# Gate and up products of a feed-forward block with the high weight against low and high input in one product of 512 columns

## The chip, the cores and the metric

The kernel runs on one core of a Trainium2 chip. The core has TensorE (matrix products into PSUM, eight banks of 512 words for each of 128 partitions), VectorE, ScalarE and GpSimd for elementwise work, and SyncE, whose queue issues nearly all loads here. The metric is the device time of one execution in microseconds. TensorE's clock is granted at one of two levels, 1.2 or 2.4 GHz; the profile gives it as a share, 0.50 or 1.00.

## The reference

Two blocks of a language model on 256 tokens of width 1024. The first is a mixer (attention beside a recurrent branch) and a gated feed-forward block, the second another mixer and a mixture of experts. The change touches the two products `h @ w_ffn_gate` and `h @ w_ffn_up`, with D_FF = 2816:

```python
def first_block(x, ...):
    ...
    x = x + rms_norm(merged @ w_o[l], norm_mix_post[l])
    h = rms_norm(x, norm_ffn_pre[l])
    f = (jax.nn.silu(h @ w_ffn_gate[l]) * (h @ w_ffn_up[l])) @ w_ffn_down[l]
    x = x + rms_norm(f, norm_ffn_post[l])
    return x
```

## The kernel before

**Split numbers.** The products of this stage run on rounded 32-bit operands (fp32r). To keep precision each operand is taken apart: a high part, which is the value rounded, and a low part, which is the value less its high part. A product is then high times high, high times low and low times high, summed in the bank (`by_parts`, lines 884 to 888, three products). The input h, transposed to 8 blocks of 128 features by 256 tokens, is held as `hT_hi[1]` (high) and `hT_lo` (low, in the place of `hT`).

**Weights.** Gate and up weights come through a ring of three slots in SBUF. A slot c holds 256 columns of gate and 256 of up, 2 MB, which is tiles f = 2c and 2c + 1; there are 11 slots, 22 tiles (KF = 22). A slot is loaded when TensorE is through with the slot three before. ScalarE writes its high part in two halves into one of three buffers (`high_parts`, line 1888), VectorE then its low part in place (`low_parts`, over line 603), 2048 words each. The slots of the down projection follow in the same ring.

**TensorE.** For tile f it makes 16 groups of three products: gate into the left half of a bank, 256 columns of the bank's 512, up into the right half. So a tile has one bank, `("ff", f)`. Banks are dealt out in a fixed list (`plan_banks`), each key the next bank of eight in turn; a key waits (`write`) until the bank's holder before it has been emptied. The down projection uses four banks, `("dn", i, n)`, and waits for all four before its first product. It also waits for `f_low`, which GpSimd writes from `f_high`.

**ScalarE and VectorE.** For each tile ScalarE takes silu of the gate half out of the bank (line 2116); VectorE multiplies it with the up half (line 2803) and the bank is free. After every second tile ScalarE rounds the two results to `f_high` (line 2121), then makes the high part of a slot three further on, and VectorE its low part. Both engines go through their lists strictly in that order. The high part of a slot can't begin before its load has landed, and the next tiles stand behind its low part on VectorE.

Of the kernel before, what the change touches and what calls it, by code (L numbers as in the profile page):

```python
# [21 lines left out]
F32 = mybir.dt.float32  # L22
# [7 lines left out]
P = 128  # L30
# [144 lines left out]
def plan_banks():  # L175
# [29 lines left out]
    o += [("mg", dm) for dm in range(KD)]  # L205
    o += [("mo", i, n) for i in range(NT) for n in range(2)]
    o += [("ad", 5)] + [("hT", 1, kk) for kk in range(4)] + [("ad", 4), ("as", 5), ("as", 4)]
    o += [("ff", m) for m in range(KF)]
    o += [("dn", i, n) for n in range(2) for i in range(NT)]
    o += [("ad", 10)] + [("x2", 0, c) for c in range(4)] + [("ad", 11), ("uz", 0, 0)]  # L210
    o += [("x2", 1, c) for c in range(4)] + [("as", 10), ("uz", 1, 0)]
# [112 lines left out]
def build(nc, A, out):  # L324
    BANK = plan_banks()
    ctx = ExitStack()
    with ctx:
# [22 lines left out]
        hT = sb("hT", [P, KD, SEQ])  # L350
        small = sb("small", [P, 616 - KD * 36 - 36 - 3 * SH - KD])
        crowded = sb("crowded", [P, 1], I32)
        ring = sb("ring", [P, RING, SLOT])
        words = nc.sbuf_bytes_remaining // 4 - 16
        arena = sb("arena", [P, words])
        where = place(words)
# [66 lines left out]
        hT_hi = {n: rounded(f"h{n}_high", [KD, SEQ], "arena", where[f"hh{n}"][0]) for n in (0, 1, 2, 3)}  # L423
        hT0_lo, hT3_lo = (rounded(f"h{n}_low", [KD, SEQ], "arena", where[f"hl{n}"][0]) for n in (0, 3))

        v_hi = [rounded(f"v_high{n}", [KD // 2, 512], "arena", where[f"hv{n}"][0]) for n in range(2)]
        osb_hi, osb_lo, orw_hi, orw_lo = (rounded(n, [PAIRS, SEQ], "arena", where[b][0]) for n, b in (
# [43 lines left out]
        def write(pe, key):  # L471

            b, turn = BANK[key]
            if turn:
                pe.wait_ge(bank_free[b], turn)
            return bank[b]

        def full(key):
            return bank_full[BANK[key][0]], 1

        def filled(eng, key):

            b, turn = BANK[key]
            eng.wait_ge(bank_full[b], turn + 1)
            return bank[b]
# [10 lines left out]
        def cols(w, c0, c1):  # L496
            return w[:, c0:c1].rearrange("(k p) c -> p k c", p=P)
# [28 lines left out]
        for c in range(KF // 2):  # L526
            if c == 1:
                modulation(4)
            stream(("ff", c), [(0, cols(A["w_ffn_gate"][0], c * 256, c * 256 + 256)),
                               (2048, cols(A["w_ffn_up"][0], c * 256, c * 256 + 256))], ("ff", 2 * c + 1))  # L530
        DOWN_K = (0, 2, 6, 10, 14, 18, KF)
        n_down = len(DOWN_K) - 1
        for c in range(n_down):
# [107 lines left out]
        def _(sp):  # L641
# [24 lines left out]
            for n, (key, parts, last) in enumerate(W):  # L666
# [37 lines left out]
                    sp.wait_ge(S("orw"), 1)  # L704
                    load_ada(5)
                if key == ("in2", 0):
                    filled(sp, ("ff", KF - 1))
# [122 lines left out]
        def _(pe):  # L830
# [53 lines left out]
            def by_parts(ps, a, b, start, stop):  # L884

                mm(ps, a[0], b[0], start=start, stop=False)  # L886
                mm(ps, a[0], b[1], start=False, stop=False)  # L887
                return mm(ps, a[1], b[0], start=False, stop=stop)  # L888

            def token_major_by_parts(key, wkey, i, high, low, ready):  # L890

# [479 lines left out]
            for f in range(KF):  # L1371
                c = f // 2
                halved(("ff", c))
                ps = write(pe, ("ff", f))
                w = parts_view(("ff", c), "p (g k c) -> p g k c", g=2, k=KD)
                for gu in range(2):
                    for k in range(KD):
                        if f == 0 and gu == 0:
                            normed(1, k)
                        last = by_parts(ps[:, gu * SEQ:(gu + 1) * SEQ], [x[:, gu, k, (f % 2) * P:(f % 2 + 1) * P] for x in w],  # L1380
                                        (hT_hi[1][:, k, :], hT_lo[:, k, :]), k == 0, k == KD - 1)
                last.then_inc(*full(("ff", f)))
            ps = {}
            for n in range(2):
                for i in range(NT):
# [465 lines left out]
        def _(act):  # L1851
# [219 lines left out]
            drained(act, ("mg", 0))  # L2071
            bcast(npost, A["norm_mix_post"][0], "npost_in")
            for dm in range(KD):
                act.wait_ge(S("merged"), dm + 1)
# [35 lines left out]
            high_parts(N_FF + 1)  # L2110
            high_parts(N_FF + 2)
            for f in range(KF):
                ps = filled(act, ("ff", f))
                if f >= 2:
                    drained(act, ("ff", f - 2))
                A_(sil[:, f % 2, :], ps[:, 0:SEQ], ACT.Silu).then_inc(S("sil"), 1)
                if f % 2:

                    drained(act, ("ff", f - 1))
                    drained(act, ("ff", f))  # L2120
                    A_(fh[:, f - 1:f + 1, :], fT[:, f - 1:f + 1, :], ACT.Copy).then_inc(S("f_high"), 1)
                    high_parts(N_FF + f // 2 + 3)
            for n in range(N_FF + KF // 2 + 3, BY_TWO + 1):
# [261 lines left out]
        def _(pool):  # L2385
# [29 lines left out]
                nc.gpsimd.tensor_copy(x.rearrange("p i h t -> p (i h) t"), eye).then_inc(S("eye"), 1)  # L2415
            for dm in range(KD):
                drained(pool, ("mg", dm))
                nc.gpsimd.tensor_tensor(gates[dm], gates[dm], gates[KD + dm], ALU.add).then_inc(S("merged"), 1)

            for c in range(KF // 2):  # L2420
                pool.wait_ge(S("f_high"), c + 1)
# [11 lines left out]
        def _(dve):  # L2433
# [24 lines left out]

            def transposed_low(s, scale, bias):

                for kk in range(4):
                    ps = filled(dve, ("hT", s, kk))
                    low_seen[0] += 1
                    dve.wait_ge(S("h_high"), low_seen[0])
                    two = slice(2 * kk, 2 * kk + 2)
                    for k2 in range(2):
                        k = 2 * kk + k2
                        cols = ps[:, k2 * SEQ:(k2 + 1) * SEQ]
                        if bias:
                            ins = V.tensor_scalar(hT[:, k, :], cols, scale(k), bias(k), ALU.mult, ALU.add)  # L2470
                        else:
                            ins = V.scalar_tensor_tensor(hT_lo[:, k, :], cols, scale(k), hT_hi[s][:, k, :].bitcast(F32), ALU.mult, ALU.subtract)  # L2472
                    if bias:
                        link(ins)
                        ins = V.tensor_tensor(hT_lo[:, two, :], hT[:, two, :], hT_hi[s][:, two, :].bitcast(F32), ALU.subtract)
                    ins.then_inc(*free(("hT", s, kk)))

            def low_parts(n):
# [319 lines left out]
            low_parts(N_FF + 1)  # L2798
            low_parts(N_FF + 2)
            for f in range(KF):  # L2800
                ps = filled(dve, ("ff", f))
                dve.wait_ge(S("sil"), f + 1)
                V.tensor_tensor(fT[:, f, :], sil[:, f % 2, :], ps[:, SEQ:2 * SEQ], ALU.mult).then_inc(*free(("ff", f)))
                if f % 2:
                    low_parts(N_FF + f // 2 + 3)
            for n in range(N_FF + KF // 2 + 3, BY_TWO):
# [498 lines left out]
```

## Time and profile before

| | us |
|---|---|
| median of 3 runs | 1091.26 |
| the runs | 1089.27 to 1091.77 |
| the profiled execution | 1090.56 |
| its span (first to last instruction) | 1088.8 |
| gate and up stage | 296.0 to 422.9 |
| down projection | 422.9 to 482.9 |
| first product of the experts | about 637 |

The span is the time between the first and the last instruction of the one execution that was profiled; 1.8 us lie around it. An engine's busy time is a sum over all stages, so a stage is read from its own stretch: which engine has no gap there, and what ended the waits of the others.

### The profile page before, as it was taken

What the parts mean: (1) busy time and instruction counts of PE and PEld (TensorE: products, weight loads), DVE (VectorE), ACT (ScalarE), POOL (GpSimd) and SP (SyncE); (2) the same over time, 40 slices, a digit from 0 to 9 for tenths busy, and PEclk for the clock granted to TensorE, in tenths of its full rate; (3) what the DMA queues carried; (4) which work ended last, traced back from release to release, by engine and by line L of the source; (5) the groups of instructions that cost most, each with busy time, mean ns of one, the idle gap of its engine ahead of it and who ended that gap; (6) DMA issues with size and microseconds to landing.
All of it is one profiled execution on the core that took longest, in us unless ns stands there. A gap on an engine that the chain in (4) does not pass through costs nothing.

```text
span 1088.8 us, 17816 instructions
## 1 busy us (share of the span) xinstructions
PE 1027.2 (94%) x7505; PEld 711.6 (65%) x7505; DVE 463.3 (43%) x704; ACT 363.8 (33%) x520; POOL 59.1 (5%) x36
## 2 busy tenths in 40 slices
PE   6999999999999999999999989999999999898987
PEld 5998779899699999877996543443444343332422
DVE  5685244658653543456886341222222222121212
ACT  6562323553644443455653421111111110110102
POOL 0004310002000010000300000000000000000000
PEclk9999999999999999999999999999999999999999
DMA  9455372048765656494539999999999999999996
GB/s 322 163 200 186 110 237 82 2 164 298 235 190 159 188 162 231 158 346 140 202 119 358 422 396 410 422 420 422 422 422 422 422 422 421 422 422 421 422 419 242
DMA packets 96406, 316.37 MB, mean 291 GB/s; under 512 B 8198, under 2 KB 33110, under 8 KB 72150
## 3 DMA queue, kind: packets, MB, share of 16 engines
q1 hardware_dynamic: 95302, 313.01, 74.7%
q10 hardware_dynamic: 1040, 2.43, 0.6%
q8 instruction: 50, 0.82, 0.3%
q14 instruction: 14, 0.11, 0.0%
HBM read 314.37 MB, written 1.05 MB: 290 GB/s over the span
## 4 chain that ended last, share of the span: by engine, by line
PE 74%; DMA 17%; DVE 2%; ACT 2%; SPq 2%; issue 2%; POOL 1%; ACTq 0%; DVEq 0%; POOLq 0%
DMA arena<-in_w 16%; PE bank L1686 14%; PE bank L886 12%; PE bank L887 11%; PE bank L888 11%; PE bank L1721 6%; PE bank L1183 3%; PE bank L869 3%; PE bank L1669 2%; PE bank L1734 1%; PE bank L1099 1%; PE bank L860 1%; DMA arena<-in_ssd_norm_w 1%; PE bank L1132 1%; PE bank L1506 1%
## 5 line engine op out<-in xcount | busy, mean ns | idle before, releaser
L1686 PE MATMUL bank<-arena,hT 128*64 128x512 f32 x576 | 225.6, 594 | 3.9 <-DMA arena<-in_w 3.9
L888 PE MATMUL bank<-h_high,ring_low 128*128 128x256 f32 x680 | 193.0, 284 | 0.0
L1686 PE MATMUL bank<-ring,hT 128*64 128x512 f32 x384 | 169.3, 594 | 11.6 <-DMA arena<-in_w 11.5
L603 DVE TENSOR_TENSOR ring_low<-ring,hi_high 128x2048 fp32r<-128x2048 f32 (+2 forms) x56 | 121.9, 2217 | 98.3 <-ACT hi_high L1888 98.1
L886 PE MATMUL bank<-h_high,hi_high 128*128 128x256 f32 x536 | 153.0, 286 | 0.5 <-DVE h_low L2472 0.5
L887 PE MATMUL bank<-h_low,hi_high 128*128 128x256 f32 x536 | 151.6, 283 | 0.0
L1888 ACT ACTIVATE hi_high<-ring 128x2048 fp32r<-128x2048 f32 (+2 forms) x58 | 104.7, 1853 | 89.9 <-DMA ring<-in_w_ffn_up 39.4
L1686 PEld LDWEIGHTS bank<-ring,hT 128*64 128x64 f32 x384 | 51.4, 137 | 122.6 <-issue 98.8
L888 PEld LDWEIGHTS bank<-h_high,ring_low 128*128 128x128 f32 x680 | 131.1, 193 | 0.0
L1721 PE MATMUL bank<-arena,ac_turned 128*64 128x512 f32 x384 | 114.9, 600 | 7.5 <-issue 7.1
L3155 DVE TENSOR_TENSOR ac<-act_of,bank 128x512 f32<-128x512 f32 x16 | 17.4, 1085 | 214.6 <-ACT act_of L2316 214.6
L886 PEld LDWEIGHTS bank<-h_high,hi_high 128*128 128x128 f32 x536 | 102.7, 192 | 2.5 <-issue 2.4
L887 PEld LDWEIGHTS bank<-h_low,hi_high 128*128 128x128 f32 x536 | 102.7, 192 | 0.3 <-issue 0.2
L1686 PEld LDWEIGHTS bank<-arena,hT 128*64 128x64 f32 x576 | 69.0, 137 | 22.9 <-issue 16.4
L2316 ACT ACTIVATE act_of<-bank 128x512 f32<-128x512 f32 x16 | 9.6, 599 | 215.6 <-PE bank L1686 215.6
L1721 PE MATMUL bank<-ring,ac_turned 128*64 128x512 f32 x128 | 58.2, 609 | 4.3 <-ACT ac_turned L2320 4.3
L1721 PEld LDWEIGHTS bank<-arena,ac_turned 128*64 128x64 f32 x384 | 35.4, 138 | 41.0 <-issue 39.6
L2325 ACT ACTIVATE y_high<-con 128x512 fp32r<-128x512 f32 x31 | 19.5, 630 | 124.5 <-DVE con L3169 119.7
L3169 DVE SCALAR_TENSOR_TENSOR con<-bank,small,arena 128x512 f32<-128x512 f32 x30 | 22.5, 751 | 82.3 <-PE bank L1721 82.3
L1721 PEld LDWEIGHTS bank<-ring,ac_turned 128*64 128x64 f32 x128 | 17.2, 140 | 38.9 <-issue 37.3
L886 PE MATMUL bank<-h_high,hrw_high 128*128 128x256 f32 x144 | 41.9, 291 | 0.0
L887 PE MATMUL bank<-h_low,hrw_high 128*128 128x256 f32 x144 | 41.5, 288 | 0.0
(441 smaller groups left out, 1727.9 us busy)
## 6 DMA issues: line engine op xcount, KB each, us to landing
arena<-in_w SPq DMA_DIRECT2D x117, 1024.0 KB, 21.9
ring<-in_w SPq DMA_DIRECT2D x63, 1024.0 KB, 17.1
ring<-in_w_in SPq DMA_DIRECT2D x12, 2048.0 KB, 7.8
ring<-in_w_ada SPq DMA_DIRECT2D x8, 2048.0 KB, 8.0
ring<-in_w_ffn_gate SPq DMA_DIRECT2D x11, 1024.0 KB, 5.4
ring<-in_w_ffn_up SPq DMA_DIRECT2D x11, 1024.0 KB, 8.0
ring<-in_w_ffn_down SPq DMA_DIRECT2D x5, 2048.0 KB, 7.8
xres<-in_w SPq DMA_DIRECT2D x8, 1024.0 KB, 23.2
```

Of the source, the lines that this page charges most:

```text
L603: return eng.tensor_tensor(ring_lo[:, r, c0:c1], ring[:, r, c0:c1], high_of(n)[:, c0:c1].bitcast(F32), ALU.subtract)
L869: last = mm(ps[:, 0:512], lhs[k][:, i * P:(i + 1) * P], w[:, k, 0:512], start=(k == 0), stop=(k == nk - 1))
L886: mm(ps, a[0], b[0], start=start, stop=False)
L887: mm(ps, a[0], b[1], start=False, stop=False)
L888: return mm(ps, a[1], b[0], start=False, stop=stop)
L1183: last = mm(ps[r, j * w:(j + 1) * w], left(4 * q + j, r), right(4 * q + j, r), start=True, stop=True)
L1669: last = mm(b[:, (k % 2) * SEQ:(k % 2 + 1) * SEQ], x[i][:, k * P:(k + 1) * P], one[:, i, :], start=(i == 0 and x is x_hi), stop=(i == NT - ...
L1686: last = mm(both(6 + half, x), hg[:, k, (2 * q + x) * CAP:(2 * q + x + 1) * CAP], w13s[q][x][c][:, k % 2, half * EF:(half + 1) * EF], star ...
L1721: last = mm(both(4 + n, x), acT[:, 0, f, x * CAP:(x + 1) * CAP], w2s[q][x][f // 2][:, f % 2, n * 512:(n + 1) * 512], start=(f == 0), stop= ...
L1888: A_(high_of(n)[:, f], ring[:, r, f], ACT.Copy).then_inc(S("high"), 1)
L2325: A_(y_hi[n], y_out[:, n, :], ACT.Copy).then_inc(S("y_high"), 1)
L3169: V.scalar_tensor_tensor(y_out[:, n, :], bank[4 + n][:, :], slot_gate[:, 0:1], g2[:, n * 512:(n + 1) * 512], ALU.mult, ALU.mult).then_inc( ...
```

## The change

One product of 512 columns takes the place of two. Where `by_parts` multiplied the high weight once with high and once with low input, the two inputs are now streamed side by side: 256 columns of low, then 256 of high, against one load of the high weight. For this the low part of h is laid ahead of the high part at a fixed distance in SBUF (`hT` is allocated after the ring, and `h1_both` is a view of both), so that one access pattern of two runs of 256 words reaches both. The left half of the bank collects high weight times low input, the right half high weight times high input, and the third product, low weight times high input, is added to the right half. Gate and up of a tile now take a full bank each, `("fg", f)` and `("fu", f)`: 44 keys and two empty places in the list of banks in the place of 22 keys.

The two halves have to be added when a bank is emptied. VectorE does it with a reduce over pairs of words 256 apart: gate into `sil`, up into `fT`. ScalarE's silu reads `sil` instead of the bank, and the multiply of VectorE reads both from SBUF. A count of finished multiplies (`rows_made`, also used by the merge stage under its old name `merged`) tells ScalarE when to round.

```diff
-    o += [("ff", m) for m in range(KF)]
+    o += [(half, m) for m in range(KF) for half in ("fg", "fu")] + [None, None]
...
+            def low_beside_high(ps, w, both, high, start, stop):
+
+                def with_high_weight():
+                    return mm(ps[:, 0:2 * SEQ], w[0], both, start=start, stop=stop)
+
+                def with_low_weight():
+                    return mm(ps[:, SEQ:2 * SEQ], w[1], high, start=False, stop=False)
+
+                if stop:
+                    with_low_weight()
+                    return with_high_weight()
+                with_high_weight()
+                return with_low_weight()
...
-                ps = write(pe, ("ff", f))
                 w = parts_view(("ff", c), "p (g k c) -> p g k c", g=2, k=KD)
                 for gu in range(2):
+                    key = (("fg", "fu")[gu], f)
+                    ps = write(pe, key)
                     for k in range(KD):
                         if f == 0 and gu == 0:
                             normed(1, k)
-                        last = by_parts(ps[:, gu * SEQ:(gu + 1) * SEQ], [x[:, gu, k, (f % 2) * P:(f % 2 + 1) * P] for x in w],
-                                        (hT_hi[1][:, k, :], hT_lo[:, k, :]), k == 0, k == KD - 1)
-                last.then_inc(*full(("ff", f)))
+                        last = low_beside_high(ps, [x[:, gu, k, (f % 2) * P:(f % 2 + 1) * P] for x in w],
+                                               h1_both[k], hT_hi[1][:, k, :], k == 0, k == KD - 1)
+                    last.then_inc(*full(key))
...
             for f in range(KF):
-                ps = filled(act, ("ff", f))
-                if f >= 2:
-                    drained(act, ("ff", f - 2))
-                A_(sil[:, f % 2, :], ps[:, 0:SEQ], ACT.Silu).then_inc(S("sil"), 1)
+                drained(act, ("fg", f))
+                A_(sil[:, f % 2, :], sil[:, f % 2, :], ACT.Silu).then_inc(S("sil"), 1)
                 if f % 2:
 
-                    drained(act, ("ff", f - 1))
-                    drained(act, ("ff", f))
+                    act.wait_ge(S("rows_made"), KD + f + 1)
                     A_(fh[:, f - 1:f + 1, :], fT[:, f - 1:f + 1, :], ACT.Copy).then_inc(S("f_high"), 1)
                     high_parts(N_FF + f // 2 + 3)
...
             for f in range(KF):
-                ps = filled(dve, ("ff", f))
+                ps = filled(dve, ("fg", f))
+                V.tensor_reduce(sil[:, f % 2, :], ps.rearrange("p (h t) -> p t h", h=2), axis=AX.X, op=ALU.add).then_inc(*free(("fg", f)))
+                ps = filled(dve, ("fu", f))
+                V.tensor_reduce(fT[:, f, :], ps.rearrange("p (h t) -> p t h", h=2), axis=AX.X, op=ALU.add).then_inc(*free(("fu", f)))
                 dve.wait_ge(S("sil"), f + 1)
-                V.tensor_tensor(fT[:, f, :], sil[:, f % 2, :], ps[:, SEQ:2 * SEQ], ALU.mult).then_inc(*free(("ff", f)))
+                drained(dve, ("fu", f))
+                V.tensor_tensor(fT[:, f, :], fT[:, f, :], sil[:, f % 2, :], ALU.mult).then_inc(S("rows_made"), 1)
                 if f % 2:
                     low_parts(N_FF + f // 2 + 3)
```

Two places of the built programs show it. TensorE, from the last products of the gate and up stage to the first of the down projection; `h1_high` and `h_low` are the parts of the input, `hi_high` and `ring_low` those of the weights. Before:

```order
L888 MATMUL bank4<-h1_high_58,ring_low_70 128x256
L886 MATMUL bank4<-h1_high_58,hi_high0_49 128x256
L887 MATMUL bank4<-h_low_69,hi_high0_49 128x256
L888 MATMUL bank4<-h1_high_58,ring_low_70 128x256
L886 MATMUL bank5<-hi_high1_50,f_high_55 128x512 [waits bank_free0,low,bank_free7,f_low,bank_free6,bank_free5]
L887 MATMUL bank5<-ring_low_70,f_high_55 128x512
```

Now:

```order
L906 MATMUL bank2<-h1_both_62,hi_high0_49 128x512
L909 MATMUL bank2<-h1_both_62,ring_low_70 128x256
L906 MATMUL bank2<-h1_both_62,hi_high0_49 128x512
L909 MATMUL bank2<-h1_both_62,ring_low_70 128x256 x2
L906 MATMUL bank2<-h1_both_62,hi_high0_49 128x512
L899 MATMUL bank5<-hi_high1_50,f_high_55 128x512 [waits bank_free0,low,bank_free7,f_low,bank_free6,bank_free5]
L900 MATMUL bank5<-ring_low_70,f_high_55 128x512
```

A group of three products of 256 columns has become one of 512 and one of 256. The first product of down waits for the same four banks (5, 6, 7, 0) as before. Their last holders were tiles 14 to 17; now they are gate and up of tile 19 (banks 5 and 6) and of tile 20 (7 and 0).

VectorE, from tile 18 to tile 20; line 603 (616 in the changed kernel) is the low part of a slot, first the short first slot of down, then its second slot. Before:

```order
L603 TENSOR_TENSOR ring_low_70<-ring,hi_high1_50 128x1024 [waits high] x2
L2803 TENSOR_TENSOR arena<-arena,bank1 128x256 [waits sil,bank_full1]
L2803 TENSOR_TENSOR arena<-arena,bank2 128x256 [waits sil,bank_full2]
L603 TENSOR_TENSOR ring_low_70<-ring,hi_high2_51 128x2048 [waits high] x2
L2803 TENSOR_TENSOR arena<-arena,bank3 128x256 [waits sil,bank_full3]
L2803 TENSOR_TENSOR arena<-arena,bank4 128x256 [waits sil,bank_full4]
```

Now:

```order
L616 TENSOR_TENSOR ring_low_70<-ring,hi_high1_50 128x1024 [waits high] x2
L2828 TENSOR_REDUCE arena<-bank3 128x256 [waits bank_full3]
L2830 TENSOR_REDUCE arena<-bank4 128x256 [waits bank_full4]
L2833 TENSOR_TENSOR arena<-arena 128x256 [waits bank_free4,sil]
L2828 TENSOR_REDUCE arena<-bank5 128x256 [waits bank_full5]
L2830 TENSOR_REDUCE arena<-bank6 128x256 [waits bank_full6]
L2833 TENSOR_TENSOR arena<-arena 128x256 [waits bank_free6,sil]
L616 TENSOR_TENSOR ring_low_70<-ring,hi_high2_51 128x2048 [waits high] x2
L2828 TENSOR_REDUCE arena<-bank7 128x256 [waits bank_full7]
L2830 TENSOR_REDUCE arena<-bank0 128x256 [waits bank_full0]
L2833 TENSOR_TENSOR arena<-arena 128x256 [waits bank_free0,sil]
```

In place of one multiply that frees a bank, a tile has two reduces, which free one bank each, and a multiply that reads SBUF. The reduces of tile 20 (banks 7 and 0) stand behind the low part of down's second slot.

## Rows read from the trace of the kernel before

**Rows 1.** The page, parts 1 and 2 (PEclk: granted clock in tenths, by slice).

```profile
span 1088.8 us, 17816 instructions
...
PE 1027.2 (94%) x7505; PEld 711.6 (65%) x7505; DVE 463.3 (43%) x704; ACT 363.8 (33%) x520; POOL 59.1 (5%) x36
...
PEclk9999999999999999999999999999999999999999
```

**Rows 2.** Groups of TensorE's instructions, 294 to 430 us: busy us, mean ns.

```profile
L886 PE MATMUL bank<-h_high,hi_high 128*128 128x256 f32 x352 | 99.8, 284 | 0.5 <-DVE h_low L2472 0.5
```

**Rows 3.** Table of stretches: the gate and up stage, the down projection.

```profile
core 0: us, PE busy (x) PEld busy (x) DVE busy (x) ACT busy (x) POOL busy (x), PEclk, DMA share, GB/s
296.00:422.90 126.90, 126.90 (x1056) 126.88 (x1057) 58.60 (x50) 56.77 (x58) 12.95 (x10) 1.00 0.55 176
422.90:482.90 60.00, 60.00 (x270) 49.41 (x270) 30.03 (x23) 24.89 (x26) 1.29 (x1) 1.00 0.74 269
```

**Rows 4.** Waits of TensorE, 426 to 640; of the load queue, 500 to 1088.

```profile
PE bank L1647 <- DVE arena L3081: 1.8, 1, 1.8
...
SPq L715 <- PE bank L1099: 9.9, 1, 9.9
```

**Rows 5.** Timeline of TensorE (start, length in us): start of down, and experts.

```profile
422.78 0.28 PE L888 MATMUL bank<-h_high,ring_low 128*128 128x256 f32 x1
422.90 0.40 PE L886 MATMUL bank<-hi_high,f_high 128*128 128x512 f32 x1
423.14 0.40 PE L887 MATMUL bank<-ring_low,f_high 128*128 128x512 f32 x1
...
652.01 0.59 PE L1686 MATMUL bank<-ring,hT 128*64 128x512 f32 x1
...
652.44 0.59 PE L1686 MATMUL bank<-ring,hT 128*64 128x512 f32 x1
```

**Rows 6.** Lines of VectorE (shortest, median, longest ns); timeline of two products.

```profile
L2803 DVE TENSOR_TENSOR arena<-arena,bank x22: 406/414/420, 310.9 to 426.1; 128x256 f32<-128x256 f32 x22
...
L3159 DVE TENSOR_REDUCE small<-bank x16: 412/424/426, 656.6 to 1070.7; 128x1 f32<-128x256 f32 x16
...
L2824 DVE TENSOR_TENSOR arena<-bank,arena x4: 679/688/694, 475.2 to 483.9; 128x512 f32<-128x512 f32 x4
...
475.25 1.28 DVE L2824 TENSOR_TENSOR arena<-bank,arena 128x512 f32<-128x512 f32 x2
```

**Rows 7.** Timeline of VectorE, 318 to 336 us.

```profile
329.69 4.49 DVE L603 TENSOR_TENSOR ring_low<-ring,hi_high 128x2048 fp32r<-128x2048 f32 x2 [5.74 <-ACT hi_high L1888]
334.10 0.75 DVE L2803 TENSOR_TENSOR arena<-arena,bank 128x256 f32<-128x256 f32 x2
```

**Rows 8.** Timeline of ScalarE, 327 to 336 us, and the silu of tile 19.

```profile
327.74 3.72 ACT L1888 ACTIVATE hi_high<-ring 128x2048 fp32r<-128x2048 f32 x2 [3.06 <-DMA ring<-in_w_ffn_up]
...
334.94 0.63 ACT L2121 ACTIVATE f_high<-arena 128x512 fp32r<-128x512 f32 x1 [2.94 <-DVE arena L2803]
...
411.58 0.38 ACT L2116 ACTIVATE arena<-bank 128x256 f32<-128x256 f32 x1 [4.24 <-PE bank L888]
```

**Rows 9.** Timeline of VectorE at the end of the stage.

```profile
421.37 4.49 DVE L603 TENSOR_TENSOR ring_low<-ring,hi_high 128x2048 fp32r<-128x2048 f32 x2 [8.88 <-ACT hi_high L1888]
425.78 0.75 DVE L2803 TENSOR_TENSOR arena<-arena,bank 128x256 f32<-128x256 f32 x2
```

**Rows 10.** Timeline of ScalarE there: high part of down's second slot.

```profile
419.42 3.72 ACT L1888 ACTIVATE hi_high<-ring 128x2048 fp32r<-128x2048 f32 x2 [6.20 <-DMA ring<-in_w_ffn_down]
```

**Rows 11.** Timeline of TensorE, two waits; table of stretches behind them.

```profile
27.50 0.39 PE L921 MATMUL bank<-con,arena 108*128 108x108 f32 x2 [2.38 <-DMA arena<-in_ssd_norm_w]
...
655.66 0.66 PE L1702 MATMUL bank<-con,ac 128*128 128x128 f32 x4 [1.76 <-DVE ac L3155]
...
28.80:32.20 3.40, 3.40 (x19) 3.40 (x18) 1.16 (x4) 0.00 (x0) 0.00 (x0) 0.50 0.98 360
656.90:660.20 3.30, 3.19 (x8) 1.00 (x10) 0.43 (x2) 0.05 (x1) 0.00 (x0) 0.50 1.02 429
```

More of the change, by code:

```diff
@@ L349, in build @@
         xres = sb("xres", [P, NT, D])
-        hT = sb("hT", [P, KD, SEQ])
         small = sb("small", [P, 616 - KD * 36 - 36 - 3 * SH - KD])
@@ L353, in build @@
         ring = sb("ring", [P, RING, SLOT])
+        hT = sb("hT", [P, KD, SEQ])
         words = nc.sbuf_bytes_remaining // 4 - 16
@@ L422, in build, with low_and_high @@
         fh, fT_lo = (rounded(n, [KF, SEQ], "arena", where[b][0]) for n, b in (("f_high", "fh"), ("f_low", "fT")))
-        hT_hi = {n: rounded(f"h{n}_high", [KD, SEQ], "arena", where[f"hh{n}"][0]) for n in (0, 1, 2, 3)}
+        hT_hi = {n: rounded(f"h{n}_high", [KD, SEQ], "arena", where[f"hh{n}"][0]) for n in (0, 2, 3)}
         hT0_lo, hT3_lo = (rounded(f"h{n}_low", [KD, SEQ], "arena", where[f"hl{n}"][0]) for n in (0, 3))
+        def low_and_high(name, low, high):
+            first, second = (start[buffer] + 4 * words for buffer, words in (low, high))
+            assert first < second
+            apart = (second - first) // 4
+            span = nc.alloc_sbuf_tensor_at(name, [P, apart + KD * SEQ], F32R, offset=first)
+            whole = span[:, 0:SEQ]
+            both = [bass.AP(tensor=whole.tensor, offset=whole.offset + k * SEQ, ap=[list(whole.ap[0]), [apart, 2], [1, SEQ]])
+                    for k in range(KD)]
+            return [span[:, c:c + KD * SEQ].rearrange("p (k t) -> p k t", k=KD) for c in (0, apart)] + [both]
+        h1_lo, hT_hi[1], h1_both = low_and_high("h1_both", ("hT", 0), ("arena", where["hh1"][0]))
         v_hi = [rounded(f"v_high{n}", [KD // 2, 512], "arena", where[f"hv{n}"][0]) for n in range(2)]
@@ L529, in build @@
             stream(("ff", c), [(0, cols(A["w_ffn_gate"][0], c * 256, c * 256 + 256)),
-                               (2048, cols(A["w_ffn_up"][0], c * 256, c * 256 + 256))], ("ff", 2 * c + 1))
+                               (2048, cols(A["w_ffn_up"][0], c * 256, c * 256 + 256))], ("fu", 2 * c + 1))
         DOWN_K = (0, 2, 6, 10, 14, 18, KF)
@@ L706, in _ @@
                 if key == ("in2", 0):
-                    filled(sp, ("ff", KF - 1))
+                    filled(sp, ("fu", KF - 1))
                     sp.wait_ge(S("down_used"), 4)
@@ L2073, in _ @@
             for dm in range(KD):
-                act.wait_ge(S("merged"), dm + 1)
+                act.wait_ge(S("rows_made"), dm + 1)
                 A_(merged_hi[:, dm, :], gates[dm], ACT.Copy).then_inc(S("merged_high"), 1)
@@ L2417, in _ @@
                 drained(pool, ("mg", dm))
-                nc.gpsimd.tensor_tensor(gates[dm], gates[dm], gates[KD + dm], ALU.add).then_inc(S("merged"), 1)
+                nc.gpsimd.tensor_tensor(gates[dm], gates[dm], gates[KD + dm], ALU.add).then_inc(S("rows_made"), 1)
             for c in range(KF // 2):
@@ L2459, in transposed_low @@
             def transposed_low(s, scale, bias):
+                low = h1_lo if s == 1 else hT_lo
                 for kk in range(4):
@@ L2471, in transposed_low @@
                         else:
-                            ins = V.scalar_tensor_tensor(hT_lo[:, k, :], cols, scale(k), hT_hi[s][:, k, :].bitcast(F32), ALU.mult, ALU.subtract)
+                            ins = V.scalar_tensor_tensor(low[:, k, :], cols, scale(k), hT_hi[s][:, k, :].bitcast(F32), ALU.mult, ALU.subtract)
                     if bias:
                         link(ins)
-                        ins = V.tensor_tensor(hT_lo[:, two, :], hT[:, two, :], hT_hi[s][:, two, :].bitcast(F32), ALU.subtract)
+                        ins = V.tensor_tensor(low[:, two, :], hT[:, two, :], hT_hi[s][:, two, :].bitcast(F32), ALU.subtract)
                     ins.then_inc(*free(("hT", s, kk)))
```

## The prediction

> **What bounds the kernel now.** I read the page first. TensorE is busy 94% of a span of 1088.8 us, VectorE 43%, ScalarE 33%, and the granted clock is near full in every slice [rows 1]. The stage that the change touches is the gate and up product of the feed-forward block. The groups of instructions in it are three lines of 352 products each, 256 columns, 1056 in all (the first of the three lines is shown, with its wait; the others have none [rows 2]), and TensorE waits ahead of them once, for 0.5 us. The table of stretches gives the stage its length: from the first product at 296.00 to the first product of the down projection at 422.90 are 126.90 us for 1056 products, 0.1202 us each; the down projection behind it takes 60.0 us for its 264 products of 512 columns, 0.2273 each [rows 3]. So TensorE sets the time here and runs without a gap, and whatever is taken off it counts, as long as nobody keeps it waiting afterwards. Behind the stage, up to 640 us, its longest single wait is 1.8 us [rows 4]: a shift of the start of down travels on to the experts. There the load queue takes up its expert loads by waiting for TensorE's products, once 9.9 us [rows 4], so the stream of expert weights, which bounds the end, moves with them. I carry every microsecond of shift to the end of the span.
>
> **The products.** The sequence for one weight tile was high times high, high times low, low times high, 256 columns each. It becomes one of 512 columns and one of 256. Columns are the same, 768. What goes is one instruction. The trace has both sizes back to back: 0.12 us from start to start for 256, 0.24 for the first of 512 [rows 5]. Over the stages it is 0.1202 and 0.2273, so two products of 256 (0.2404) against one of 512 (0.2273) save 0.0131 us. With 22 x 2 x 8 = 352 weight tiles that is 352 x 0.0131 = 4.6 us. Both sizes carry about the same 13 ns beyond their columns at 2.4 GHz (106.7 and 213.3 ns), which is why one instruction less is worth 13 ns. The products with 64 columns of weights in the experts come every 0.43 us in pairs of 512 columns [rows 5], about 0.215 each: there the extra is some 2 ns. A 512-column product with a full weight tile in the trace has its 13, and I take that row, since it is the same form.
>
> The Trainium skill (TensorE: Matmul & The Clock Gate, section Back-to-back issue gap) gives N/2.4 + 2.5 ns from one product to the next for a single isolated one. By it alone an instruction less would be worth 2.5 ns, 0.9 us in all; the rows here show 13. What would follow if the changed pair came down to that gap is rival D.
>
> The new stage on TensorE: 352 x (0.1202 + 0.2273) = 122.3 us, or 11.12 for one weight slot (32 pairs) against 11.54.
>
> **The drain.** Before, one bank held gate and up of a tile; ScalarE took silu out of it and VectorE multiplied, 0.414 us a tile [rows 6], a pair taking 0.75 [rows 7]. Now there are two full banks, each emptied by a reduce of 512 words to 256. No such reduce is in the trace. Its nearest rows: a reduce of 256 words from a bank into one takes 0.424 us, as much as the product of 256 from a bank (0.414), and a product of 512 words from a bank takes 0.688, the second of two starting 0.60 after the first (1.28 for two) [rows 6]. I take 0.69, next one 0.60 later. From below it can't cost less than the 0.42 of half the words; from above, if writing 256 results came on top of reading 512, 0.69 + 0.33 = about 1.0. The tile's chain is then: reduce of gate at 0, of up at 0.60, done at 1.29; silu, which waits for the gate only, 0.38 [rows 8], done at about 1.2, beneath the second reduce; the multiply at 1.33, and the next tile at 1.66. Two tiles take 3.4 us instead of 0.75, 2.65 more. Over the stage VectorE goes from 58.6 busy us [rows 3] to some 85 of 122: no bound by share.
>
> It sits in a loop, though. VectorE empties the two tiles, ScalarE rounds the result (f_high), and only then makes the next slot's high half, which VectorE needs for the low half, behind which stand the next two tiles. From the rows: high part to first low part 327.74 to 329.69 = 1.95, low part to drain 329.69 to 334.10 = 4.41 [rows 7, 8], drain 3.4, f_high and its handover 0.7. Sum 10.5 us, under the 11.12 of a slot. ScalarE now waits for the weights 3.06 us before a high part [rows 8]; the 2.65 eat into that and leave 0.4. Inside the stage this costs nothing: the low part of a slot is ready some 8 us before TensorE comes to it (one is ready at 334.1 [rows 7], for the slot that begins at 296.0 + 4 x 11.54 = 342.2), and a bank is used again two slots later.
>
> **The end of the stage is where I see the price.** The four banks of down (5, 6, 7, 0) are all waited for before its first product. Before, their last holders were tiles 14 to 17. Now they are gate and up of tiles 19 and 20 (the order of the change, ahead). Tile 20 is drained by VectorE behind the low part of the second down slot, and that part was finished at 425.8, 2.9 us after down had begun, with tiles 20 and 21 multiplied only then [rows 9]. Nobody minded. Now TensorE will. The chain: tenth slot done at 296.0 + 10 x 11.12 = 407.2 (before 411.4; the load behind it lands and ScalarE starts its high part at 419.42, 8.0 later [rows 10]). So high part at 415.2, low part at 417.2, its end 421.6, gate of tile 20 emptied from there, up of tile 20 done 1.29 later at 422.9, TensorE 0.1 later (a handover here: the multiplies end at 334.85, f_high starts at 334.94 [rows 7, 8]): down starts at 423.0. TensorE itself is done with the stage at 418.3. It stands 4.7 us, and down starts 0.1 later than the 422.90 of before. The whole 4.6 us goes into this wait.
>
> **The clock.** After a wait of 2.38 us ended at 27.50 the granted clock was 0.50 (1.2 GHz) from 28.8 to 32.2; after a wait of 1.76 that ended at 655.66, again 0.50 for 656.9 to 660.2; with the single 0.5 us before the stage it stayed at 1.00 [rows 11, 3, 2]. The new wait of 4.7 us is longer than either. One spell like that is 3.4 us of products at half speed, of which 1.7 us are lost; none would be 0, two in a row 3.4. The down projection runs without slack on TensorE, so I put all of it on the path: 1.7.
>
> **Sum.** -4.6 (products) + 4.7 (wait) + 1.7 (clock) = +1.8. Against the profiled execution's own 1090.56 that is 1092.4. The three timed runs lie at 1089.27 to 1091.77, mean 1090.8, so I say 1092.6 for the median.
>
> **Rivals.** *A2, the clock takes longer to come back*: the fall comes while TensorE waits and again after its restart, 3.4 us lost, 1094.1. For it: the wait is twice those of the trace. Against: both spells seen ended after one. *A0, no fall*: 1090.7. Against: waits of 2.38 and 1.76 us had one. *B, the reduce is dearer and the loop becomes the bound (the slower side)*: at 1.0 us from start to start the drain takes 5.0 and the loop 12.1, from 11.12 on every 0.1 of it counts; 1.0 us a slot over nine slots, 9.0 late less the 0.4 spare, and the last drain comes at about 431: 1092.4 + 8 = 1100. The point is a reduce of 0.75 us start to start. For it: a read that jumps 256 words for each output and an output for every two words, neither in the trace. Against: the reduce and the product of 256 words from a bank cost the same 0.42, so the words read seem to set it. *C, the change doesn't meet that wait* (the banks are free in time): 1090.56 - 4.6 = 1086.0. Against: the order of banks and of VectorE says otherwise. *D, the pair is cheaper than its parts*: a weight load hidden under 512 columns takes its 13 ns off both products, a pair 0.325 instead of 0.3475, a slot 10.4, so the loop's 10.5 rules: tenth slot done at 296.0 + 105 = 401.0, down 15.8 behind it at 416.8 (as 423.0 stands to 407.2), 6.1 before the old 422.90, and with 1.7 of clock 1090.56 - 6.1 + 1.7 = 1086.2. For it: the 64-column weights have only 2 ns. Against: 512 columns in down have their 13. The skill's gap above would give such a pair.
>
> **How the numbers follow.** Forecast (one spell) 0.47, A2 0.18, A0 0.10, B 0.10, C 0.05, D 0.10. About 0.2%, 2.2 us, is what a measurement of this kernel tells from no change. Faster by that: C, D and a little of the rest, 0.15. Slower, over 1093.0 against 1090.8: A2, B, and a fifth of the forecast by its scatter, 0.38. Same 0.47. The range takes the forecast, A0, A2, with 1.5 us of run scatter below, and the lower part of B: 1088.5 to 1098. Left out are C, D and the far part of B.
>
> **What would show it.** In the changed profile: TensorE's slots 11.1 us apart; one wait of 4 to 5 us before the first down product, ended by a VectorE reduce; down's start within 1 us of 422.9; granted clock 0.5 for some 3 us behind it; the reduce at 0.69. Wrong would be: no such wait (C), waits in every slot (B), slots under 10.8 us (D), full clock after the wait (A0).

## The result

| | median us | runs | range |
|---|---|---|---|
| before | 1089.21 | 22 | 1087.02 to 1092.02 |
| changed | 1093.25 | 22 | 1089.01 to 1095.91 |

The ratio is 1.0032, with a 95% interval of 1.0020 to 1.0043: the change makes the kernel slower by 0.32%, some 3.5 us. The measured median is 0.65 us above the predicted 1092.6 and inside the range, but by the 0.2% bound this is "slower" (given 0.38) and not "same" (0.47). That the median came so close is in part luck: the kernel before took 1089.21 in these runs, 1.6 us less than the 1090.8 from which the forecast started. The change itself was forecast at 1.8 us and measured at 3.5 by the ratio, 4.0 by the medians.

The page of the changed kernel (parts 1 and 2), against [rows 1]:

```profile
span 1091.3 us, 17125 instructions
...
PE 1028.6 (94%) x7153; PEld 695.2 (64%) x7153; DVE 491.4 (45%) x748; ACT 366.5 (34%) x520; POOL 58.8 (5%) x36
...
PEclk9999999999999998999999999999999999999999
```

The span is 2.5 us longer, TensorE issues 352 products less, and the granted clock has one slice below 9, the sixteenth, where the down projection starts.

The table of stretches: the gate and up stage, the first 5 us of down, the rest of it, and two short stretches, at 592 and at 633. The rows of the kernel before are in [rows 3]:

```profile
core 0: us, PE busy (x) PEld busy (x) DVE busy (x) ACT busy (x) POOL busy (x), PEclk, DMA share, GB/s
294.21:418.50 124.29, 124.29 (x704) 107.83 (x704) 84.13 (x90) 59.05 (x58) 12.94 (x10) 1.00 0.56 180
423.28:428.20 4.92, 4.92 (x12) 3.87 (x13) 1.76 (x4) 2.83 (x3) 1.28 (x1) 0.50 0.51 208
428.30:485.30 57.00, 57.00 (x253) 47.18 (x252) 26.12 (x19) 21.20 (x21) 0.00 (x0) 1.00 0.67 244
592.20:595.50 3.30, 3.30 (x6) 1.24 (x5) 2.53 (x6) 0.21 (x1) 0.00 (x0) 0.50 1.05 405
633.10:636.40 3.30, 3.30 (x5) 1.35 (x4) 2.85 (x15) 1.48 (x2) 0.00 (x0) 0.50 1.00 417
```

The stage now goes from 294.21 to the first down product at 423.28: 129.07 us, where it was 126.90. TensorE works through 124.3 of them at full clock and stands for the rest. Down goes from 423.28 to 485.34, 62.06 us in place of 59.64 (measured to its last product's start, 482.54 before), and its first 5 us are at clock 0.50. The end of the stage on TensorE (start, length) beside [rows 5]:

```profile
416.76 0.40 PE L906 MATMUL bank<-h_both,hi_high 128*128 128x512 f32 x1
417.00 0.28 PE L909 MATMUL bank<-h_both,ring_low 128*128 128x256 f32 x1
417.12 0.40 PE L906 MATMUL bank<-h_both,hi_high 128*128 128x512 f32 x1
417.36 0.28 PE L909 MATMUL bank<-h_both,ring_low 128*128 128x256 f32 x1
...
423.28 0.77 PE L899 MATMUL bank<-hi_high,f_high 128*128 128x512 f32 x1 [4.59 <-DVE arena L2830]
...
428.41 0.39 PE L899 MATMUL bank<-hi_high,f_high 128*128 128x512 f32 x1
```

A wide product starts 0.24 us ahead of the next one, a short one 0.12. Then TensorE stands 4.59 us for line 2830, VectorE's reduce of up. Down's products are at half clock (0.50, 1.2 GHz) until about 428.2, and the row of 428.41 has the old length again. A stretch at half clock is called a spell below. ScalarE and VectorE there, against [rows 9, 10]:

```profile
415.25 3.72 ACT L1916 ACTIVATE hi_high<-ring 128x2048 fp32r<-128x2048 f32 x2 [3.48 <-DMA ring<-in_w_ffn_down]
...
417.19 4.49 DVE L616 TENSOR_TENSOR ring_low<-ring,hi_high 128x2048 fp32r<-128x2048 f32 x2 [6.10 <-ACT hi_high L1916]
421.61 0.68 DVE L2828 TENSOR_REDUCE arena<-bank 128x256 f32<-128x512 f32 x1
422.21 0.68 DVE L2830 TENSOR_REDUCE arena<-bank 128x256 f32<-128x512 f32 x1
422.99 0.42 DVE L2833 TENSOR_TENSOR arena<-arena 128x256 f32<-128x256 f32 x1
```

High part 415.25, low part 417.19, then the two reduces of tile 20, of which the second ends at 422.89; TensorE's first product starts 0.4 later, at 423.28. The reduce itself, over all 22 tiles, in ns, shortest, median and longest:

```profile
L2828 DVE TENSOR_REDUCE arena<-bank x22: 676/684/686, 308.5 to 423.3; 128x256 f32<-128x512 f32 x22
```

**Where the 2.5 us of the two profiled executions are**, by places at which TensorE passes: it comes to the stage 1.79 us earlier (294.21 against 296.00; nothing of the change lies ahead of it, and the stage starts of the other kernels below scatter between 292.7 and 296.1); the stage takes 2.17 more, down 2.42 more, the way from there to the experts 1.71 more (156.88 against 155.17), and the experts with the end 2.00 less (449.1 against 451.1). In the 1.71 are two further spells at clock 0.50, at 592.2 and 633.1 in the table above, neither of which the kernel before has there; it has one at 656.9 instead [rows 11], inside the experts, where the changed kernel has none. (Before, TensorE also waited 1.8 us for VectorE on that way [rows 4]; in the changed kernel it doesn't, so the two spells show with less than their 3.3.) The profiles of the other kernels below have spells between 588 and 660 too, one or two each, with a wait at down and without one, so I count these as scatter. That is not proven by one profile each: the one other kernel that waits at down has its two at 593 and 634 as well. By this count two terms, 2.17 and 2.42, belong to the change: 4.6 us in this execution.

### The profile page after: what moved, and what is told of

Same layout as the page of the kernel before. It is cut to its first block, busy times and chain, and to the rows that moved or that the text cites. A ratio compares the mean times of both kernels' runs of the same rounds, so it can differ in the third digit from the quotient of the medians.

```text
span 1091.3 us, 17125 instructions
## 1 busy us (share of the span) xinstructions
PE 1028.6 (94%) x7153; PEld 695.2 (64%) x7153; DVE 491.4 (45%) x748; ACT 366.5 (34%) x520; POOL 58.8 (5%) x36
## 3 DMA queue, kind: packets, MB, share of 16 engines
q10 hardware_dynamic: 1040, 2.43, 0.6%
## 4 chain that ended last, share of the span: by engine, by line
PE 73%; DMA 17%; DVE 2%; ACT 2%; SPq 2%; issue 2%; POOL 1%; ACTq 0%; DVEq 0%; POOLq 0%
DMA arena<-in_w 16%; PE bank L1714 14%; PE bank L899 8%; PE bank L900 7%; PE bank L901 7%; PE bank L906 7%; PE bank L1749 6%; PE bank L909 3%; PE bank L1210 3%; PE bank L882 3%; PE bank L1697 2%; PE bank L1762 1%; PE bank L1126 1%; PE bank L873 1%; PE bank L1159 1%
## 5 line engine op out<-in xcount | busy, mean ns | idle before, releaser
L906 PE MATMUL bank<-h_both,hi_high 128*128 128x512 f32 x352 | 121.2, 398 | 0.5 <-DVE h_both L2498 0.5
L901 PE MATMUL bank<-h_high,ring_low 128*128 128x256 f32 x328 | 93.4, 285 | 0.0
L909 PE MATMUL bank<-h_both,ring_low 128*128 128x256 f32 x352 | 91.6, 281 | 0.0
L906 PEld LDWEIGHTS bank<-h_both,hi_high 128*128 128x128 f32 x352 | 63.2, 188 | 13.5 <-issue 1.3
L909 PEld LDWEIGHTS bank<-h_both,ring_low 128*128 128x128 f32 x352 | 66.5, 189 | 4.1
L901 PEld LDWEIGHTS bank<-h_high,ring_low 128*128 128x128 f32 x328 | 63.5, 193 | 0.0
L899 PE MATMUL bank<-h_high,hi_high 128*128 128x256 f32 x184 | 53.2, 289 | 0.0
L900 PE MATMUL bank<-h_low,hi_high 128*128 128x256 f32 x184 | 52.0, 282 | 0.0
```

Source lines behind the costliest of these rows:

```text
L906: return mm(ps[:, 0:2 * SEQ], w[0], both, start=start, stop=stop)
L909: return mm(ps[:, SEQ:2 * SEQ], w[1], high, start=False, stop=False)
```

## The experiments

The theory: the wide product saves something, but its two banks a tile make the start of down wait for VectorE, and that wait brings a spell at half clock; both together are more than the saving. Rivals: the added work of VectorE and ScalarE costs TensorE something all along the stage; or the difference comes from other stages.

**Down takes banks that are empty earlier.** Its four banks become those of tiles 18 and 19.

```diff
-    o += [(half, m) for m in range(KF) for half in ("fg", "fu")] + [None, None]
-    o += [("dn", i, n) for n in range(2) for i in range(NT)]
+    o += [(half, m) for m in range(KF) for half in ("fg", "fu")]
+    o += [("dn", i, n) for n in range(2) for i in range(NT)] + [None, None]
```

> The changed kernel with the two empty places of the bank list moved behind the four banks of down, so that down takes the banks of tiles 18 and 19, emptied some 8 us before TensorE is through. My theory (the 4.6 us wait for tile 20's bank and the clock spell behind it are the loss): no wait of TensorE at the start of down, down starts 124.3 us after the stage's first product (129.1 in the changed kernel, 126.9 before), no half clock there, and the time is 2.6 us below the kernel before (ratio 0.9976) and 7 below the changed one. Rival (the loss comes from the stage itself, by VectorE's 28 us of added work or from other stages): the wait turns up elsewhere, at a low half of a weight slot, and the ratio stays near 1.003.

Measured: 1086.37 us median of 12 runs against 1088.78, ratio 0.998 (0.9966 to 0.9993). TensorE's timeline at the start of down, VectorE's reduce of tile 20, and the stretches of stage and down:

```profile
419.97 0.40 PE L909 MATMUL bank<-h_both,ring_low 128*128 128x256 f32 x2
420.21 0.40 PE L906 MATMUL bank<-h_both,hi_high 128*128 128x512 f32 x1
420.44 0.40 PE L899 MATMUL bank<-hi_high,f_high 128*128 128x512 f32 x1
...
423.37 0.68 DVE L2828 TENSOR_REDUCE arena<-bank 128x256 f32<-128x512 f32 x1
...
296.12:420.30 124.18, 124.17 (x704) 107.84 (x705) 84.17 (x90) 59.05 (x58) 12.93 (x10) 1.00 0.55 180
420.44:480.10 59.66, 59.66 (x265) 49.36 (x263) 32.12 (x27) 24.91 (x25) 1.29 (x1) 1.00 0.74 269
```

Down follows the last wide product without a wait, 124.32 us after the stage's first product, although VectorE begins to empty tile 20 only at 423.37, 3 us into down. The clock stays at 1.00 and down takes 59.6 us again. The loss turned into a gain by moving two empty places in a list: the rival of a cost along the stage falls, and this version is faster than both kernels.

**The same with three products.** It leaves everything of the run above but the wide product.

```diff
-                    return mm(ps[:, 0:2 * SEQ], w[0], both, start=start, stop=stop)
+                    mm(ps[:, 0:SEQ], w[0], both[:, 0, :], start=start, stop=False)
+                    return mm(ps[:, SEQ:2 * SEQ], w[0], both[:, 1, :], start=False, stop=stop)
```

> As e1_banks, but the product of 512 columns is made as two of 256 into the two halves of the bank: 1056 products as before, with banks, reduces and order of the changed kernel. It prices the wide product alone, against e1_banks. My theory: slots 11.54 us apart, down 126.9 us after the first product, no wait, time equal to the kernel before within 0.1%. Rival (two banks a tile and the reduces cost TensorE something by themselves): slots above 11.54 and a ratio above 1.001.

Measured: 1088.70 (12 runs) against 1088.78, ratio 0.9994 (0.998 to 1.0007). The stage's stretch, and the longest of TensorE's waits from 290 to 430 us:

```profile
294.75:421.60 126.85, 126.85 (x1056) 126.82 (x1057) 84.34 (x90) 59.34 (x58) 12.94 (x10) 1.00 0.55 177
...
PE bank L906 <- DVE h_both L2499: 0.5, 1, 0.5
```

1056 products, 84.3 us of VectorE's work instead of 58.6 [rows 3], and the stage takes 126.91 us from first product to down, the 126.90 of before. So the second bank and the reduces cost nothing inside the stage, and the wide product by itself is worth 126.91 - 124.32 = 2.6 us, not 4.6.

**The kernel before, with the wait.** Only down's banks are moved, so that one of them is tile 20's.

```diff
-    o += [("ff", m) for m in range(KF)]
-    o += [("dn", i, n) for n in range(2) for i in range(NT)]
+    o += [("ff", m) for m in range(KF)] + [None] * 3
+    o += [("dn", i, n) for n in range(2) for i in range(NT)] + [None] * 5
```

> The kernel before with three empty places ahead of down's banks in the list and five behind, so that one of the four is that of tile 20, whose multiply ends at 426.2 in the trace of before. Nothing else differs. My theory: TensorE waits 3.4 us for that multiply, the clock falls to 0.50 for one or two spells behind it (1.7 to 2.5 us lost), ratio 1.0047 to 1.0055. Rival (the clock does not follow from the wait): 3.4 us alone, ratio 1.003; rival (the wait is made up later, behind down): ratio under 1.001.

Measured: 1096.81 (6 runs) against 1088.78, ratio 1.0067 (1.0048 to 1.0085), 7.3 us by the ratio. Timeline, clock behind the wait, and one more wait, 60 us on:

```profile
420.30 0.28 PE L888 MATMUL bank<-h_high,ring_low 128*128 128x256 f32 x1
424.07 0.77 PE L886 MATMUL bank<-hi_high,f_high 128*128 128x512 f32 x1 [3.50 <-DVE arena L2803]
424.63 0.63 PE L887 MATMUL bank<-ring_low,f_high 128*128 128x512 f32 x1
...
424.00:429.20 5.20, 5.13 (x12) 4.10 (x13) 0.04 (x1) 1.29 (x2) 1.28 (x1) 0.50 0.70 287
...
PE bank L1099 <- DVE arena L2824: 1.0, 1, 1.0
```

A wait of 3.50 us, then clock 0.50 until 430, about 6 us of products of which 3.0 are lost, and 1.0 us that the edit itself brings: a later product has got a bank that VectorE reads for down's end. Sum 7.5, measured 7.3. A bank list alone, without the change, makes the kernel slower by more than the change did. My 1.0047 to 1.0055 had left out the 1.0 and had the spell half a microsecond too short.

**The wait filled with work.** TensorE waits as in the changed kernel, but is busy.

```diff
+            halved(("down", 0))
+            pe.wait_ge(S("f_low"), DOWN_K[1] // 2)
+            filler = parts_view(("down", 0), "p (k c) -> p k c", k=DOWN_K[1])
+            for turn in range(20):
+                mm(ps[turn % 2, 0][:, 0:512], fh[:, 0, 0:P], filler[0][:, 0, 0:512], start=True, stop=True)
```

> The changed kernel with 20 extra products of 512 columns (4.55 us of work whose results are overwritten) issued into down's first two banks, which are free, before TensorE waits for the other two. The wait for tile 20 stays, TensorE is busy during it. My theory: down's real products start at the same place as in the changed kernel, 129.1 us after the first product, but at full clock: 2.5 us less than the changed kernel there, ratio about 1.001. Rival (the clock costs nothing at the end of the span): same time as the changed kernel, ratio 1.0032.

Measured: 1091.24 (12 runs) against 1088.78, ratio 1.0023 (1.0011 to 1.0035).

```profile
416.99 4.70 PE L1418 MATMUL bank<-hi_high,f_high 128*128 128x512 f32 x20
421.53 0.39 PE L899 MATMUL bank<-hi_high,f_high 128*128 128x512 f32 x1
421.76 0.40 PE L900 MATMUL bank<-ring_low,f_high 128*128 128x512 f32 x1
...
421.50:428.00 6.50, 6.50 (x30) 5.39 (x30) 3.12 (x5) 4.14 (x4) 1.29 (x1) 1.00 0.41 169
```

The 20 products, whose results nobody uses, end as VectorE does; down's first real one starts at 421.53, 128.87 us after the stage's first (292.66), about where it did in the changed kernel (129.07), and at full clock. In the profile that takes the 2.4 us off down. Over the runs the gain is smaller: the ratios, 1.0023 and 1.0032, differ by 1.0 us, and the medians lie 2.5 and 4.0 us above those of the kernel before that ran beside them. The intervals overlap, so the times alone don't prove that the clock's share reaches the end of the span. The granted clock of all runs points the same way: on average 0.9930 in the 22 runs of the changed kernel, 0.9952 in these 12, 0.9949 in 29 of the kernel before.

**VectorE empties tile 20 first.** The banks stay as in the change, the order is turned.

```diff
+                if f == KF - 3:
+                    emptied(KF - 2)
                 if f % 2:
                     low_parts(N_FF + f // 2 + 3)
```

> The changed kernel with its own banks, but VectorE empties tile 20 before it makes the low part of down's second slot, not after. It takes the same wait away from the other end. My theory: tile 20 is empty some 5 us before TensorE is through, no wait, full clock, down 124.3 us after the first product, ratio 0.998 as e1_banks. Rival (what e1_banks gained hung on the other banks, not on VectorE's order): the wait stays near 4.6.

Measured: 1085.12 (6 runs) against 1089.15, ratio 0.9964 (0.995 to 0.9978). VectorE's timeline, then TensorE's:

```profile
411.81 0.68 DVE L2829 TENSOR_REDUCE arena<-bank 128x256 f32<-128x512 f32 x1
414.23 0.69 DVE L2831 TENSOR_REDUCE arena<-bank 128x256 f32<-128x512 f32 x1 [1.74 <-PE bank L906]
418.25 4.49 DVE L616 TENSOR_TENSOR ring_low<-ring,hi_high 128x2048 fp32r<-128x2048 f32 x2 [3.33 <-ACT hi_high L1916]
422.67 0.42 DVE L2838 TENSOR_TENSOR arena<-arena 128x256 f32<-128x256 f32 x1
...
419.44 0.40 PE L906 MATMUL bank<-h_both,hi_high 128*128 128x512 f32 x1
419.67 0.40 PE L899 MATMUL bank<-hi_high,f_high 128*128 128x512 f32 x1
```

The reduces of tile 20 (411.81 and 414.23) stand ahead of the low part (418.25), its multiply behind; down starts at 419.67, 124.31 after the first product. The same as with other banks, from the other side: the wait was the order of VectorE's list against the bank list.

**Why the wide product saved 2.6 and not 4.6.** Three experiments ask what makes it take 0.235 us in this stage when it took 0.2273 in down. Grouped: in each bank the eight wide products first, then the eight short ones.

```diff
+                    for k in range(KD):
...
+                        mm(ps[:, 0:2 * SEQ], sides[0][k], h1_both[k], start=(k == 0), stop=False)
+                    for k in range(KD):
+                        last = mm(ps[:, SEQ:2 * SEQ], sides[1][k], hT_hi[1][:, k, :], start=False, stop=(k == KD - 1))
```

> As e1_banks (down's banks free early), but in each bank the eight products of 512 columns come first and the eight of 256 after them, instead of by turns. It asks why a pair took 0.353 us in the changed kernel and not 0.3475. If the turns between the two lengths cost (each 512 after a 256 or the other way), slots fall from 11.30 to 11.12 us, down starts 122.3 us after the first product in place of 124.3, ratio 0.996. If they don't, all stays at 124.3 and 0.998.

Measured: 1084.63 (11 runs) against 1089.15, ratio 0.9964 (0.9953 to 0.9974), the lowest median of the kernels that were timed more than once. TensorE, eight products a row: the stage's first bank, then one in the middle of it.

```profile
294.43 3.00 PE L1409 MATMUL bank<-h_both,hi_high 128*128 128x512 f32 x8 [0.49 <-DVE h_both L2500]
...
320.57 2.00 PE L1409 MATMUL bank<-h_both,hi_high 128*128 128x512 f32 x8
322.41 1.11 PE L1411 MATMUL bank<-h_both,ring_low 128*128 128x256 f32 x8
```

Eight wide ones take 2.00 us, with the last one's 0.39 off 1.61 for seven steps: 0.230 each; the short ones (1.11 - 0.28) / 7 = 0.119. Down starts 123.91 us after the first product, 0.4 less than by turns, not 2.0. But the 0.4 is the rest of a gain and a loss. From bank to bank the grouped kernel takes 2.793 us where turns take 2.820, which is 0.3492 a pair in place of 0.3525, or 1.15 us over the 43 banks behind the first, and a slot comes to 11.17 where 11.12 was expected. The first bank, though, takes 3.79 us instead of 3.06: its eight wide products start in pairs, some 0.78 us from pair to pair, while VectorE writes the eight blocks of the low input one every 0.39 us; by turns the short products lie in that time. So the turns do cost, about two thirds of what a pair takes beyond the forecast 0.3475. The ratio is not apart from the 0.9964 and 0.998 of the kernels that keep the turns; all this is a reading of the trace.

One run of 512 words in place of two of 256 (all blocks but the first then leave out high weight times low input, and put the high input of the block before in its place, so the output is wrong):

```diff
-                    return mm(ps[:, 0:2 * SEQ], w[0], both, start=start, stop=stop)
+                    return mm(ps[:, 0:2 * SEQ], w[0], h1_run[k - 1] if k else both, start=start, stop=stop)
```

> As e1_banks, but the 512 columns are one run of 512 words out of the high parts (block k - 1 and block k) for k over 0, in place of two runs of 256 words lying far apart; the products then leave out high times low, and the work is of the same size. If the two runs cost the extra 5.7 ns a pair, down starts 122.6 us after the first product; if not, 124.3.

```profile
294.09:418.30 124.21, 124.21 (x704) 107.84 (x705) 83.81 (x90) 58.65 (x58) 12.96 (x10) 1.00 0.56 180
```

The stretch ends at the last products; down starts at 418.43, 124.34 after the first one. Where the words lie makes no difference. Measured in one run: 1083.97 us.

Wide products alone, without low weight times high input:

```diff
-                if stop:
-                    with_low_weight()
-                    return with_high_weight()
-                with_high_weight()
-                return with_low_weight()
+                return with_high_weight()
```

> As e1_banks, without the products of the low weight part (352 products of 512 columns are left, none of 256; the output lacks that part). It asks why a 512-column product of this stage takes 0.231 to 0.240 us and one of down 0.227. If the short products between them are the cause, all come down to 0.227, a slot is 32 x 0.227 = 7.3 us for TensorE and the weights' way through ScalarE and VectorE becomes the bound, at 10.5 us a slot or a little more. If it is the operands of this stage, the products inside a bank stay at 0.231 or above.

Measured in one run, 1069.12 us beside 1090.78. TensorE inside a slot, the sum of its waits for the reduce of gate, and ScalarE's high parts slot by slot:

```profile
345.82 2.43 PE L906 MATMUL bank<-h_both,hi_high 128*128 128x512 f32 x10
...
PE bank L906 <- DVE arena L2824: 15.4, 7, 2.9
...
342.41 3.71 ACT L1912 ACTIVATE hi_high<-ring 128x2048 fp32r<-128x2048 f32 x2
...
352.87 3.71 ACT L1912 ACTIVATE hi_high<-ring 128x2048 fp32r<-128x2048 f32 x2
...
363.32 3.71 ACT L1912 ACTIVATE hi_high<-ring 128x2048 fp32r<-128x2048 f32 x2
```

Ten wide products in a row take 2.43 us, 0.227 a step. So the operands of this stage stream as fast as those of down; it is the company of short products that costs. In this run the first wide product behind a wait starts 0.31 us ahead of the next at full clock, five to nine behind it 0.224 to 0.236, and only those that follow a steady 0.226 to 0.227. The first five products of down in the kernel before have the same 0.228 to 0.236. In groups of eight the last three get to 0.227; by turns the starts go on between 0.224 and 0.241, at 0.235 in the median. What in the engine does that stays open.

The same run puts the loop to the test, since TensorE needs only 7.3 us a slot: the high parts start 10.46 and 10.45 us apart, and now TensorE waits for reduces in seven slots, 15.4 us in all.

## Why the prediction was right or wrong

**What bounds the kernel.** Right: behind the first product TensorE has no wait of note in the stage, in any version that keeps all its products.

**The products, 4.6 us.** Wrong in size: 2.6. The step that failed was to take the 0.2273 of down's unbroken row of wide products as the price of one among short ones. A pair takes 124.3 / 352 = 0.3532 and not 0.3475, with the short one at about 0.12, so the wide one costs about 0.235; slots are 11.28 us apart, not 11.12. The last experiment shows in what company the wide one costs that, and the grouped one wins two thirds of it back from bank to bank. The bound from the row of 64-column weights, and with it rival D, pointed the wrong way. It was also a misreading: the two products of such a pair start 0.01 us apart (637.71 and 637.72 in the trace of before), side by side, so 0.215 is half the step of a pair and not a distance between products.

**The Trainium skill's gap** (TensorE: Matmul & The Clock Gate, section Back-to-back issue gap; N/2.4 + 2.5 ns) gave, as an estimate, 0.9 us for one instruction less. The measured 2.6 lies between it and my 4.6; in the stage a wide and a short product together keep 32 ns beyond their columns (0.3525 less 0.3200 us), not 5, so the rule's own figure is not seen here.

**The drain.** Right: a reduce of 0.684 and 0.680 us, starts 0.60 apart, two tiles in 3.5 us (421.61 to 424.72 + 0.43) where 3.4 were forecast, and the loop 10.46 against the 10.5 of the sum. Rival B needed 0.75 from start to start and fell with this.

**The wait, 4.7 us.** Right in place, cause and size: 4.59 by the trace, ended by the reduce of up, and 4.75 as the stage's 129.07 less the 124.32 that it takes without it. Its chain starts at the tenth slot's end (the high part follows 8.0 us behind it, as forecast), so most of the missing 2.0 us of saving came through to down, and the handover from VectorE took 0.39 and not 0.1: down starts 2.17 later relative to the stage and not 0.1.

**The clock, 1.7 us.** Right that it falls. I had counted one spell of 3.4 us of work. In the profile the clock was at 0.50 from 421.4 to 428.2, two such lengths, of which the first 1.9 us lay under the wait and TensorE worked the last 4.96: down took 2.42 us longer. That is the picture of rival A2, at a lower price than its 3.4. But the profiled execution is one of the six with the lowest mean granted clock of the 22, 0.990. Over the runs it varies: those six took 1093.1 to 1095.9 us, the four with 0.997 took 1089.0 to 1090.3. The 3.5 to 4.0 us of all runs, less 4.75, plus 2.6, leave 1.3 to 1.9 for the clock on average, an estimate that has the 1.7 in it.

The argument for the fall was weaker than it looked. "Waits of 2.38 and 1.76 us had one" leaves out the wait of 1.78 us that ended at 632.72 in the same trace [rows 4]: the clock stayed at 1.00 behind it, from 633 to 638. And in the grouped kernel a wait of 2.59 us, at the place where 2.38 had a spell before, had none:

```profile
27.74 0.39 PE L948 MATMUL bank<-con,arena 108*128 108x108 f32 x2 [2.59 <-DMA arena<-in_ssd_norm_w]
...
28.00:32.00 4.00, 4.00 (x36) 4.00 (x35) 1.20 (x4) 0.69 (x2) 0.00 (x0) 1.00 0.89 330
```

So a wait of 1.8 to 2.6 us brings a spell in some places and executions and none in others, and by [rows 4] A0 deserved more than its 0.10.

**Sum.** -2.6 + 4.75 + 2.4 = +4.6 in the profiled execution; over all runs 3.5 by the ratio and 4.0 by the medians. The forecast was -4.6 + 4.7 + 1.7 = +1.8. It had the right mechanism; the term of the products was mis-sized by 2.0 us, and that took the result across the 0.2%.

## What to carry to other kernels

When a change makes a stage take more banks, look at who holds the banks that the *next* stage waits for first, and behind what their emptying stands: here two empty places in a list decided between 0.32% slower and 0.2% faster, and so did one change in the order of VectorE's work (0.36% faster). A saving upstream of such a wait is only worth what it moves the chain that ends the wait. And price an instruction by a row where it stands in the same company, not by one in an unbroken row of its own kind.

## What the runs showed of the hardware

A wait of 3.5 us at the start of down was followed by 6.8 us at half clock (423.3 to 430.1 in the kernel before with the wait), one of 4.59 us by 6.8 as well (421.4 to 428.2 in the changed kernel; the spell began under the wait in both), twice as long as the spells behind the 2.38 and 1.76 us waits [rows 11] in the kernel before. Waits of 1.78 and 2.59 us in two other places of the traces were followed by none. With TensorE kept busy on results that nobody uses, the spell at down did not come. That is one profile, in which the 1.92 us wait near 27 us had no spell either; the mean granted clock of its 12 runs, 0.9952 against 0.9930, speaks for the same. Wide products (512 columns) start 0.227 us apart in a long unbroken row and 0.224 to 0.241 apart among short ones, in a pattern that repeats from bank to bank.
